# Rotary embedding in a fused decoder trunk: the half swap of q and k by four DMA copies inside the on-chip memory, in place of a matrix product

## The reference, cut to what matters

```python
def apply_rope(x, cos, sin):
    x1, x2 = jnp.split(xf, 2, -1)          # 32 and 32 features of each part of 64
    return jnp.concatenate([x1 * cos - x2 * sin, x2 * cos + x1 * sin], -1)

s = jnp.einsum('bqhcd,bkhcd->bhcqk', q_blk, k) * scale      # two maps per head, causal
p = jax.nn.softmax(s, axis=-1);  p = p[:, :, 0] - lam * p[:, :, 1]
o = rms_norm(p @ v, subln_w) * (1.0 - lambda_init)
```

## Time and profile before

| | |
|---|---|
| median of 3 runs | 1631.45 us |
| profiled execution | 1633.52 us, its span 1631.8 us |
| PE / PEld busy | 1513.1 us (93%) / 1222.3 us (75%) |
| DVE busy | 948.3 us (58%) |
| ACT / POOL busy | 668.1 us (41%) / 132.5 us (8%) |
| granted TensorE clock, mean | 0.975 |
| DMA, mean | 77 GB/s |

### The profile page before, as it was taken

How to read it: one execution, slowest core, us unless ns; L and a number is a source line. 1 busy time by engine, 2 the same in 40 slices (tenths; PEclk the granted TensorE clock), 3 DMA queues, 4 the chain that set the end, 5 groups by cost and what they waited for, 6 DMA issues and landing times.

```text
span 1631.8 us, 21054 instructions
## 1 busy us (share of the span) xinstructions
PE 1513.1 (93%) x7429; PEld 1222.3 (75%) x7429; DVE 948.3 (58%) x1351; ACT 668.1 (41%) x954; POOL 132.5 (8%) x133
## 2 busy tenths in 40 slices
PE   6999999999886799999999899999868999999998
PEld 5788877888674688888788686656556888887886
DVE  5655665466444665666522725889877666666226
ACT  4542344334312455555411234554532555555211
POOL 3311221122100000000000001111100000000000
PEclk8999999999997999999999999999979999999999
DMA  5211110111022333333332231111133333333331
GB/s 159 54 38 40 39 51 26 39 43 48 27 65 65 117 91 102 103 90 97 109 103 91 75 107 39 39 39 51 51 103 90 117 100 92 99 94 93 113 101 67
DMA packets 158813, 125.10 MB, mean 77 GB/s; under 512 B 5995, under 2 KB 145709, under 8 KB 158765
## 3 DMA queue, kind: packets, MB, share of 16 engines
q1 hardware_dynamic: 154832, 119.55, 24.3%
q10 hardware_dynamic: 3932, 4.89, 0.9%
HBM read 122.33 MB, written 2.10 MB: 76 GB/s over the span
## 4 chain that ended last, share of the span: by engine, by line
PE 78%; DVE 12%; ACT 4%; issue 3%; DMA 2%; ACTq 1%; DVEq 0%
PE bank L1365 14%; PE bank L1367 14%; PE bank L1366 14%; PE bank L1422 9%; PE bank L1353 6%; PE bank L1354 6%; PE bank L1355 6%; DVE w_lo L300 2%; ACT w_hi L295 2%; PE bank L1683 1%; DVE att_std L1224 1%; DMA raw<-in_diff_w_out 1%; DVE x_tok L1073 1%; DVE bn L1077 1%; PE bank L1383 1%
## 5 line engine op out<-in xcount | busy, mean ns | idle before, releaser
L300 DVE TENSOR_TENSOR w_lo<-raw,w_hi 128x1024 fp32r<-128x1024 f32 x220 | 273.0, 1245 | 359.2 <-ACT w_hi L295 355.7
L1365 PE MATMUL bank<-x_hi,w_hi 128*128 128x512 f32 (+1 forms) x1120 | 452.5, 404 | 15.5 <-DVE x_lo L844 11.1
L1367 PE MATMUL bank<-x_hi,w_lo 128*128 128x512 f32 (+1 forms) x1120 | 432.2, 386 | 0.0
L1366 PE MATMUL bank<-x_lo,w_hi 128*128 128x512 f32 (+1 forms) x1120 | 431.0, 385 | 0.0
L295 ACT ACTIVATE w_hi<-raw 128x1024 fp32r<-128x1024 f32 x220 | 230.2, 1052 | 221.2 <-PE bank L1355 153.6
L1365 PEld LDWEIGHTS bank<-x_hi,w_hi 128*128 128x128 f32 x1120 | 212.1, 189 | 56.6 <-DVE x_lo L844 11.8
L1367 PEld LDWEIGHTS bank<-x_hi,w_lo 128*128 128x128 f32 x1120 | 211.6, 189 | 43.1
L1366 PEld LDWEIGHTS bank<-x_lo,w_hi 128*128 128x128 f32 x1120 | 212.4, 190 | 38.7 <-issue 3.6
L1353 PE MATMUL bank<-w_hi,u_hi 128*128 128x512 f32 x480 | 197.1, 411 | 46.6 <-DVE w_lo L300 35.1
L1355 PE MATMUL bank<-w_hi,u_lo 128*128 128x512 f32 x480 | 192.8, 402 | 0.0
L1354 PE MATMUL bank<-w_lo,u_hi 128*128 128x512 f32 x480 | 192.7, 401 | 0.0
(11 more groups left out here) (242 smaller groups left out, 1892.5 us busy)
## 6 DMA issues: line engine op xcount, KB each, us to landing
raw<-in_ffn_w_up SPq DMA_DIRECT2D x88, 512.0 KB, 3.8
raw<-in_ffn_w_down SPq DMA_DIRECT2D x44, 512.0 KB, 3.2
raw<-in_gdn_w_in SPq DMA_DIRECT2D x32, 512.0 KB, 4.0
raw<-in_diff_w_in SPq DMA_DIRECT2D x24, 512.0 KB, 3.7
raw<-in_gdn_w_out SPq DMA_DIRECT2D x16, 512.0 KB, 3.4
raw<-in_diff_w_out SPq DMA_DIRECT2D x16, 512.0 KB, 3.3
x_tok<-in_x SPq DMA_DIRECT2D x4, 512.0 KB, 6.3
out_x<-x_tok SPq DMA_DIRECT2D x3, 512.0 KB, 2.7
```

The source lines that it names most:

```text
L300: nc.vector.tensor_tensor(w_lo[:, s, :], raw[:, (base + r) % RAW, :], w_hi[:, s, :].bitcast(F32), ALU.subtract).then_inc(lo_ready, 1)
L1365: nc.tensor.matmul(out, hi, x_hi[:, k, cols], start=(k == 0), stop=False)
L1366: nc.tensor.matmul(out, hi, x_lo[:, k, cols], start=False, stop=False)
L1367: ins = nc.tensor.matmul(out, lo, x_hi[:, k, cols], start=False, stop=last)
```

## The change

`rotate` and its two calls per head go from PE. Instead SP issues, for q and for k of each head, four DMA copies of 32 partitions x 512 float32 (64 KB each) from `qk_raw` to a new tile `qk_rot`, with the halves exchanged. The sign moves into the sine pass: a column `turn_sign` (computed once, on DVE, from the matrix `swap`) multiplies in a scalar_tensor_tensor that reads `qk_rot` in place of the bank. ACT's `take` waits in addition until the copies of the head before have landed. SP's loop over the q and k loads is written out, so that the copies stand between the loads.

```diff
-            with sp.Fori(0, PAIRS) as it:
-                for r in range(4):
-                    load(C_QK, it, r, tile_of(w_att, (r % 2) * D + (2 * it + r // 2) * P))
...
+            def swap_halves(g, kind):
+
+                wait_read(sp, kind, T_QK // 2 + g)
+                sp.wait_ge(rope_head, R_DVE0 - RD_N + RD_N * g + RD["rope2 " + "qk"[kind]])
+                for b in range(4):
+                    to, src = b * P // 4, (b ^ 1) * P // 4
+                    sp.dma_start(qk_rot[kind][to:to + P // 4, :],
+                                 qk_raw[kind][src:src + P // 4, :]).then_inc(rot_loaded[kind], 16)
+
+            for r in range(5):
+                load_qk(0, r)
+            for kind in range(2):
+                swap_halves(0, kind)
+            for h in range(HEADS - 3):
+                load_qk(h, 5)
+                load_qk(h, 6)
+                for kind in range(2):
+                    swap_halves(h + 1, kind)
...
                 if not (isinstance(g, int) and g == 0):
                     act.wait_ge(rope_pool, 2 * g + kind - 1)
+                    act.wait_ge(rot_loaded[kind], 64 * g)
...
+            dve.wait_ge(masks_ready, N_MASKS)
+            nc.vector.tensor_reduce(turn_sign[:, :], swap[:, :], AX.X, ALU.add, negate=True).then_inc(lam_dve, 1)
...
-                dve.wait_ge(rot_pe, 2 * g + kind + 1)
-                nc.vector.tensor_tensor(rope2[kind][:, :], bank[4 + kind][:, :], sin[:, :], ALU.mult).then_inc(rope_head, 1)
+                dve.wait_ge(rot_loaded[kind], 64 * g + 64)
+                nc.vector.scalar_tensor_tensor(rope2[kind][:, :], qk_rot[kind][:, :], turn_sign[:, 0:1], sin[:, :],
+                                               ALU.mult, ALU.mult).then_inc(rope_head, 1)
...
-            def rotate(g, kind):
-
-                wait_read(pe, kind, T_QK // 2 + g)
-                nc.tensor.matmul(bank[4 + kind][:, :], swap[:, :], qk_raw[kind][:, :], start=True,
-                                 stop=True).then_inc(rot_pe, 1)
-
...
-                if not last:
-                    rotate(h + 1, 0)
...
-                if not last:
-                    rotate(h + 1, 1)
```

More of the change, by code:

```diff
@@ L163, in build @@
         eps = sb("eps", [P, 3])
+        turn_sign = sb("turn_sign", [P, 1])
         lamv = sb("lamv", [P, 4, HD])
@@ L212, in build @@
         vh = place("uh", 9, "vh", [P, NT, P])
+        qk_rot = [place("uh", 11 + i, f"qk_rot{i}", [P, T]) for i in range(2)]
         Eb = [[place("ul", 2 * i + c, f"Eb{i}{c}", [P, T]) for c in range(2)] for i in range(2)]
@@ L248, in build @@
         t_pe, t_dve, t_act, v_head = sem("t_pe"), sem("t_dve"), sem("t_act"), sem("v_head")
-        rot_pe, rope_pool, rope_head = sem("rot_pe"), sem("rope_pool"), sem("rope_head")
+        rot_loaded, rope_pool, rope_head = [sem("rot_loaded0"), sem("rot_loaded1")], sem("rope_pool"), sem("rope_head")
         n_sq, n_sum, n_std, n_dve = sem("n_sq"), sem("n_sum"), sem("n_std"), sem("n_dve")
@@ L357, in _, with load_qk, load_att_out @@
                 load_rows(C_V + k, w_att, k, D, 2 * D)
-            with sp.Fori(0, PAIRS) as it:
-                for r in range(4):
-                    load(C_QK, it, r, tile_of(w_att, (r % 2) * D + (2 * it + r // 2) * P))
-            for p_ in range(2):
-                for k in range(HEADS):
-                    load_rows(C_ATT_OUT + HEADS * p_ + k, a["diff_w_out"][0], k)
+            def load_qk(h, r):
+                c = C_QK + 2 * h + r
+                sp.wait_ge(lo_ready, c - RAW + 1)
+                src = tile_of(w_att, (r % 2) * D + (h + r // 2) * P)
+                dst = raw[:, (C_QK + r) % RAW, :].rearrange("p (k n) -> p k n", k=KT)
+                sp.dma_start(dst, src).then_inc(raw_loaded[(C_QK + r) % RAW], 16)
+            def load_att_out(k):
+                load_rows(C_ATT_OUT + k, a["diff_w_out"][0], k % HEADS)
+            def swap_halves(g, kind):
[14 more added lines that the diff above has]
+                    swap_halves(h + 1, kind)
+            load_qk(HEADS - 3, 5)
+            load_att_out(0)
+            for kind in range(2):
+                swap_halves(HEADS - 2, kind)
+            load_att_out(1)
+            load_att_out(2)
+            for kind in range(2):
+                swap_halves(HEADS - 1, kind)
+            for k in range(3, 2 * HEADS):
+                load_att_out(k)
             load_up(1)
@@ L1737, in _ @@
             pe.wait_ge(v_out, 2 * NT)
-            rotate(0, 0)
-            rotate(0, 1)
             step(0, 0)
@@ L1802 @@
 ROPE_DVE = 18
-LAM_DVE = 5
+LAM_DVE = 6
 INPUTS = ["x", "positions", "gdn_w_in", "gdn_conv_w", "gdn_a_log", "gdn_dt_bias", "gdn_norm_w", "gdn_w_out",
```

## The result

| | before | after |
|---|---|---|
| median | 1630.82 us (4 runs, 1630.12 to 1635.01) | 1655.07 us (4 runs, 1653.95 to 1656.92) |
| ratio to before, 95% interval | | 1.0144 (1.0125 to 1.0164) |
| profiled execution, span | 1631.8 us | 1652.2 us |
| granted clock, mean of the runs | 0.975 (profiled execution) | 0.969 to 0.972 |

The change makes the kernel 24 us slower. The prediction was 11 us slower, 1642.4 us, with a range up to 1651.0: the direction is right, the size is less than half of what came.

What follows compares the result with a forecast made beforehand. DVE's row was taken to bound the heads: 1.40 us k wait plus 0.06 sine pass over 7 heads, 10.2, plus 0.8 in head 0, 11.0 us, giving 1642.4 us on the median; range 1633.5 to 1651.0.

Steps and rivals of the forecast that it cites:

- The bound and the direction: Attention heads: DVE's row of instructions, not PE, sets a head's end, so waiting for k copies makes the kernel slower.
- q's copies: SP's q copies in heads 1 to 7: landed by about 1090.3, before DVE wants them at 1091.72, so hidden.
- B: Rival: PE is the bound, so removing the k rotation wins 7.1 us in heads 1 to 7, 1624.3; chance 0.04.
- A: Rival: the copies are hidden, no difference; 1632.7, at most 1635.8 with POOL's hold-up of rope2 k; chance 0.11.
- The issue term: SP's four k copies: 0.40 us per issue, bounds 0.37 and 0.47, the fourth starting 1.20 us after the first.
- The landing term: k copies in heads 1 to 7: the last lands 2.1 us after its issue, bounds 1.5 and 2.7.
- The sine pass: DVE's rope2 as scalar_tensor_tensor: 0.75 instead of 0.69, +0.06 us per head, paid in full for k, not for q.
- Head 0: First head: q copies land late behind the fifth load, plus two sine passes; +0.8 us taken, +0.2 to +1.3.
- rival C: TensorE's clock falls as PE idles longer in each head; 3 us per head, 21 us more, 1663; chance 0.08.
- The estimates of the gaps: PE's idle times per head after the change: 2.4 us before the transposes, 2.4 before the scores, both below 3.20.

Runs made afterwards that it cites:

- e3: Changed kernel with both rotation matrix products also kept on PE, their results unused; 1648.43 us, ratio 1.0112 to the kernel before.
- e5: e3 with two of k's four copies issued by ACT instead of SP; 1639.18 us, ratio 1.0054 to the kernel before.
- e7: e2 with q's matrix product also kept on PE, its result unused; 1633.62 us, ratio 1.0006 to the kernel before.
- e8: e3 with k's four transfers reading a DRAM tensor of the same shape, k's swapped tile left out; 1644.22 us, ratio 1.0065.
- e6: Changed kernel without copies or rotation products, the sine pass reading qk_raw, halves not exchanged; 1635.81 us, ratio 1.0018.
- e4: Changed kernel with one copy of 128 partitions in place of each four of 32, halves not exchanged; 1644.82 us, ratio 1.0085.
- e1: Changed kernel with only k copied, q rotated by the matrix product on PE as before; 1657.57 us, ratio 1.0170.
- e2: Changed kernel with only q copied, k rotated by the matrix product on PE as before; 1635.35 us, ratio 1.0022.
- v1: Kernel before with one q add of 128 partitions instead of two of 64, scores reading 64-row operands; 1649.75 us, ratio 1.0111.
- v4: Kernel before with POOL's k multiply after the qz pair, two projection products and the k rotation moved earlier on PE; 1634.23 us, ratio 1.0011.

## Why the prediction was right and wrong

**The bound and the direction: right.** DVE's row sets a head's end. The k copies end last, rope2 q never waits in heads 1 to 7 of after (in e3, e5, e7 and e8 it waits 0.22 to 0.53 us in one head or two), and the scores wait for `kr`, as in the earlier trace rows. e7 shows q's copies at nearly nothing, e6 that the removal of the matrix products gives nothing. B is false, A too.

**The issue term: mis-sized, beyond its bound.** "I take 0.40, of the smallest transfers", upper bound 0.47. It is 0.59 to 0.61, so the fourth issue starts 1.8 us after the first, not 1.2. The rows named as nearest were nearest in size; they read DRAM, and e8 shows that this makes 0.17 us of difference at the same shape. e5 shows that the term works as the sum had it.

**The landing term: right.** 2.1 taken, about 2.05 measured for the last k copy. The Trainium skill's "SBUF — State Buffer", section "The DMA setup-cost knee (why "@ 1 MiB" ≠ asymptote)", was the source of the prediction's estimate of 2.15 us, which is 0.1 above the measured; its advice of one large transfer agrees with the runs too, e4 being 10 us below after.

**The sine pass: less than half of its price.** Predicted +0.06. The instruction is 0.75, but the next one starts 0.87 after it, where before it was 0.73 (1094.95 to 1095.68): +0.14. Together, from the end of `take` to rope2 k 3.90 - 2.00 = 1.90, and 0.14, make 2.04 of the 2.07 us per head that e3 shows; the prediction had 1.46. Over seven heads 14.4 us in place of 10.2, inside its own range of 5.4 to 15.9.

**Head 0: +0.8 predicted, 2.7 came.** From POOL's first multiply to rope2 q it is 7.21 us against 5.57: +1.64, the upper bound. 0.40 came back because POOL's k multiply was over. Then PE's gap ahead of the first scores was 4.25 us, before 1.17, and the clock fell behind it: +1.47 us up to L1338. That is a clean price of one fall: from the end of `kr` to L1338 head 0 takes 21.33 to 21.36 us in the six runs with a fall there (after, e1, e3, e4, e7, e8) and 19.88 or 19.89 in the three without (before, e2, e5).

**The step that failed is the clock, rival C.** It got a chance of 0.08 because "Both are below 3.20", the one gap for which I had shown a fall. The estimates of the gaps were fair: 2.4 and 2.4, measured 2.20 and 2.69. The use of 3.20 as a threshold was the error: one observed fall says nothing about shorter gaps. This term alone puts the result outside the range: e3, with every other cost of the change in it and head 0's fall too, is at 1648.43, inside 1633.5 to 1651.0. The trace of before had the answer in another stage, in rows that the prediction does not have (PE's timeline, and a window):

```profile
455.76 0.79 PE L1353 MATMUL bank<-w_hi,u_hi 128*128 128x512 f32 x1 [2.65 <-DVE w_lo L300]
```

```profile
456.00:460.00 4.00, 4.00 (x16) 3.38 (x17) 0.96 (x2) 1.01 (x1) 0.00 (x0) 0.61 0.73 225
```

A fall behind 2.65 us. C's size, 21 us, was too large by its price: 3 us for each fall, where head 0 shows 1.47. The heads of e1 have a fall each, and the first six are 1.4 to 1.6 us longer than e3's, but for one that is 3.1 longer. What the runs show in place of nothing: 6.6 us by the medians of after and e3, six falls behind fourteen gaps. The rule of the Trainium skill that I had cited for it ("TensorE: Matmul & The Clock Gate", section "HAM oscillation — how this bites in real kernels") agrees in its mechanism, a fall in every pass of a loop that waits for a DMA; e1 shows one in each of the seven heads. I gave it too little weight.

**What adds up.** In the profiled executions the stage grew by 28.2 us: 14.4 for the copies in heads 1 to 7 with the clock held, 2.7 in head 0 (1.47 of it the clock), and 11.1 for what after has above e3 in heads 1 to 7. The span grew by less, 20.4 us, since what lies ahead of the stage ran 6.2 us shorter in that execution (granted clock 0.98, before 0.97) and what lies behind it 1.6. Of the last head's +5.8 us, 2.0 is in e3 too. The rest begins with a fall at the transposes, and one of its k copies took 1.71 us to issue, about 1.1 more than the others; why, no run tells. So some 10 of the 11.1 us are the clock's, in this pair of executions; the medians give 6.6.

What stays open: why one gap of 2.2 or 2.7 us ends in a fall and the next does not. Ahead of head 0's scores PE was idle for 2.47 us in e7 and 2.79 in e5, and these are the windows behind it, first e7, then e5:

```profile
992.00:996.00 4.00, 4.00 (x13) 2.87 (x13) 2.10 (x8) 2.88 (x9) 0.00 (x0) 0.57 0.00 0
```

```profile
992.00:998.00 6.00, 5.29 (x28) 3.74 (x29) 4.15 (x11) 3.03 (x10) 0.00 (x0) 1.00 0.00 0
```

The clock fell behind the shorter one and held behind the longer, so the length alone doesn't decide.

## What to carry to other kernels

Add up the whole chain from the producer's end to the consumer, every serial issue of its own, and take issue times from rows with the same source memory and the same number of partitions; four small copies cost three issues more than one. A product that stands ahead of a wait of TensorE is not free to remove: look at the granted clock behind every gap of the length that would result, in all stages of the trace. Where three chains end together, none of them is worth shortening alone.

## What the runs showed of the hardware

- Issuing a 64 KB DMA of 32 partitions on SP takes 0.59 us from SBUF and 0.42 us from DRAM; one of 128 partitions, 256 KB, from SBUF 0.47 us. On ACT's queue two of the first kind take 1.34 us, on SP's 1.14 (e5).
- The TensorE clock fell to its lower level (products of 0.63 us in place of 0.39) behind idle times of 2.20 us, and not behind all of these: behind 2.20 in four heads of seven in e2. One fall costs 1.47 us in head 0.
- 64-row products between 128-row ones (v1): 2.60 us where the 128-row form takes 1.72, for four products and four masks.
- A DVE instruction with two SBUF operands beside POOL's multiply: the pair of qz 2.38 and 2.49 us, alone 1.40 (e4, v4); rope2 1.67 in place of 0.75 (e6). The Trainium skill's "SBUF — State Buffer", section "Who interferes with whom", says so: two SBUF inputs contend with a GpSimd instruction that reads SBUF.
